# A weight ring of three slots of eight k-tiles, and another split of work between VectorE, ScalarE and GpSimd in the up projection

## What is computed

```python
xn = rmsnorm(x, p['norm_mix_g'])
proj = (xn @ p['w_in'] + p['b_in']).astype(f32)
...   # GLA, mLSTM and RG-LRU branches from slices of proj
mix = (g3[:, :, 0] * (o_gla @ wb[:GLA_V]) + g3[:, :, 1] * (o_m @ wb[GLA_V:GLA_V + M_WIDTH])
       + g3[:, :, 2] * (o_r @ wb[GLA_V + M_WIDTH:]))
x = (x.astype(f32) + mix @ p['w_out'].astype(f32)).astype(dt)
xn2 = rmsnorm(x, p['norm_ffn_g'])
u = (xn2 @ p['w_up']).astype(f32)
uc, fconv_new = causal_dwconv(u, fconv.astype(f32), p['ffn_conv_w'].astype(f32), p['ffn_conv_b'].astype(f32))
u_a, u_b = jnp.split(uc, 2, axis=-1)
x = (x.astype(f32) + (jax.nn.gelu(u_a) * u_b) @ p['w_down'].astype(f32)).astype(dt)
```

## Time and profile before

| | us |
|---|---|
| median of 3 runs (1105.35 to 1109.82) | 1105.7 |
| span of the profiled execution | 1107.9 |
| TensorE busy in it | 1037.6 (94%) |
| VectorE, ScalarE, GpSimd busy | 657.3, 372.1, 346.7 |
| mean granted TensorE clock | 0.978 |
| low parts on GpSimd, 121 of them | 341.2 |
| the two later taps on VectorE, 88 of them | 106.7 |

### The profile page before, as it was taken

One profiled execution on the slowest core, in us unless ns is written; L12 is line 12 of the kernel. 1 busy time (PEld: TensorE's weight loads), 2 busy tenths in 40 slices (PEclk: granted clock), 3 DMA queues, 4 the chain that ended last, 5 costly groups with the idle time before them and its releaser, 6 DMA issues.

```text
span 1107.9 us, 19962 instructions
## 1 busy us (share of the span) xinstructions
PE 1037.6 (94%) x7812; PEld 983.0 (89%) x7812; DVE 657.3 (59%) x1051; ACT 372.1 (34%) x518; POOL 346.7 (31%) x144
## 2 busy tenths in 40 slices
PE   6989999999788999998999999989999999899996
PEld 5979878889787999887999999989999999799995
DVE  4373224457995445657455668888888888531322
ACT  5633333244644454413332332222222222221121
POOL 3333121123221322322342323334433333333330
PEclk9989999999999999999899989999999999999998
DMA  5135212124222222433422322222322223322312
GB/s 152 44 91 124 58 41 66 44 57 114 81 57 58 77 58 58 116 105 95 138 76 69 82 72 76 76 76 78 88 81 84 86 76 90 98 68 84 100 52 81
DMA packets 165766, 89.34 MB, mean 81 GB/s; under 512 B 7508, under 2 KB 163802, under 8 KB 165681
## 3 DMA queue, kind: packets, MB, share of 16 engines
q1 hardware_dynamic: 151493, 79.16, 25.9%
q10 hardware_dynamic: 14222, 9.47, 3.1%
HBM read 82.29 MB, written 6.32 MB: 80 GB/s over the span
## 4 chain that ended last, share of the span: by engine, by line
PE 53%; DVE 25%; issue 13%; POOL 2%; DVEq 2%; ACT 2%; DMA 1%; ACTq 1%; POOLq 0%
PE ps L547 41%; DVE ca L1923 8%; PE ps L536 2%; DVE ca L1919 2%; POOL wlo L495 2%; DVE hp L1931 1%; DVE up L1904 1%; DVE up L1905 1%; PE ps L651 1%; PE ps L647 1%; DVE rt L1688 1%; PE ps L738 1%; PE ps L678 1%; DMA xtok<-x_prompt 1%; PE ps L819 1%
## 5 line engine op out<-in xcount | busy, mean ns | idle before, releaser
L495 POOL TENSOR_TENSOR wlo<-stage,whi 128x1024 fp32r<-128x1024 f32 (+2 forms) x121 | 341.2, 2821 | 734.0 <-ACT whi L1006 452.2
L547 PE MATMUL ps<-xh,whi 128*128 128x272 f32 x1552 | 329.8, 294 | 22.7 <-POOL wlo L495 19.5
L547 PE MATMUL ps<-xh,wlo 128*128 128x272 f32 x1552 | 322.5, 289 | 0.0
L547 PE MATMUL ps<-xl,whi 128*128 128x272 f32 x1552 | 322.4, 289 | 0.0
L547 PEld LDWEIGHTS ps<-xh,whi 128*128 128x128 f32 x1552 | 245.9, 190 | 34.9 <-POOL wlo L495 22.4
L547 PEld LDWEIGHTS ps<-xl,whi 128*128 128x128 f32 x1552 | 246.1, 190 | 0.0
L547 PEld LDWEIGHTS ps<-xh,wlo 128*128 128x128 f32 x1552 | 244.7, 190 | 0.0
L1006 ACT ACTIVATE whi<-stage 128x1024 fp32r<-128x1024 f32 (+2 forms) x59 | 72.4, 1229 | 179.1 <-PE ps L547 175.4
L1923 DVE SCALAR_TENSOR_TENSOR ca<-up,par,ca 128x560 f32<-128x560 f32 x88 | 106.7, 1213 | 12.7
L1015 ACT ACTIVATE whi<-stage 128x1024 fp32r<-128x1024 f32 (+1 forms) x54 | 59.4, 1101 | 77.0 <-PE ps L547 77.0
L547 PE MATMUL ps<-hh,whi 128*128 128x272 f32 x352 | 74.4, 293 | 5.3 <-DVE hl L1935 3.1
(11 more groups left out here) (386 smaller groups left out, 1449.8 us busy)
## 6 DMA issues: line engine op xcount, KB each, us to landing
stage<-w_in SPq DMA_DIRECT2D x52, 512.0 KB, 4.0
stage<-w_up SPq DMA_DIRECT2D x44, 512.0 KB, 3.8
...
stage<-w_out SPq DMA_DIRECT2D x8, 512.0 KB, 3.6
ch<-state_mlstm_C ACTq DMA_DIRECT2D x4, 512.0 KB, 4.2
s_mlstm_C<-ch ACTq DMA_DIRECT2D x4, 512.0 KB, 3.2
...
```

The lines of the kernel that those rows point to most:

```text
L495: pool.tensor_tensor(wlo[:, slot, 0:kt], stage[:, slot, 0:kt], whi[:, slot, 0:kt].bitcast(F32), ALU.subtract).then_inc(s("lo"), 1)
L547: ins = mm(dst[:, r, :], w[:, slot, k0 + k, :], x(k)[:, r * HT:(r + 1) * HT], start=first and k == 0 and q == 0, stop=last and k == n - 1 ...
```

## The change

- `stage`, `whi` and `wlo` have three slots of eight k-tiles in the same space. A load waits for the low part of unit u-3, `hi` until TensorE has used unit u-3 (`used`, `split_made` give the semaphore and value).
- Units of the gated branches become three for two n: two gate units of eight k-tiles, and one with the two branch tiles of four k-tiles side by side (36 units in place of 24). TensorE counts them with `gate_mm` and `br_mm`. On ScalarE `hi` of the next pair's gate stands right behind the gate's sigmoid, ahead of `visit(u, 1)`; `hi` of the branch unit only behind every second n.
- Down projection: units of 8, 8 and 6 k-tiles, three per output tile (24 in place of 16); TensorE waits for `hl` 8, 16, 22.
- Up projection: from the third up unit on, VectorE makes the low parts (`up_lo`, semaphore `lo_up`), and ScalarE the first tap (`first_tap`, an Identity with scale and bias, semaphore `tap0`). VectorE's order in a step is now: evict, `hl` of the step before (r = 0), low part, two taps; then `hp`. ScalarE's is: `hi`, first tap, `gelu`, `hi`, first tap, `up_hi`.
- The first unit's matmuls use 68 weight columns, not 128; the out projection's loops are written out.

The diff, cut to its core:

```diff
 U_SMALL, U_QKV, U_MU, U_RX, U_RY, U_GG, U_MO, U_GB = 0, 1, 9, 13, 17, 21, 25, 29
-U_OUT = U_GB + 3 * KD
+U_OUT = U_GB + 9 * KD // 2
 U_UP = U_OUT + KD
 U_DOWN = U_UP + 2 * NF
-U_END = U_DOWN + 2 * KD
-KT_IN, KT_GB, KT_DOWN, KT_MAX = 8, 12, 11, 12
+U_END = U_DOWN + 3 * KD
+SLOTS, KT = 3, 8
+KT_DOWN = (8, 8, 6)
+U_DVE = U_UP + 2
+N_GB = U_OUT - U_GB
...
 def kt_of(u):
-    return KT_GB if U_GB <= u < U_OUT else KT_DOWN if u >= U_DOWN else KT_IN
+    return KT_DOWN[(u - U_DOWN) % 3] if u >= U_DOWN else KT
+
+
+def used(u):
+
+    if U_GB <= u < U_OUT:
+        i, j = divmod(u - U_GB, 3)
+        return ("gate_mm", 2 * i + j + 1) if j < 2 else ("br_mm", 2 * i + 2)
+    return "gemm", u + 1 - (N_GB if u >= U_OUT else 0)
+
+
+def split_made(u):
+
+    if U_DVE <= u < U_DOWN:
+        return "lo_up", u - U_DVE + 1
+    return "lo", u + 1 - (U_DOWN - U_DVE if u >= U_DOWN else 0)
...
-        stage = at("stage", [P, 2, KT_MAX, P], 0)
-        whi = at("whi", [P, 2, KT_MAX, P], 12288, F32R)
-        wlo = at("wlo", [P, 2, KT_MAX, P], 24576, F32R)
+        stage = at("stage", [P, SLOTS, KT, P], 0)
+        whi = at("whi", [P, SLOTS, KT, P], 12288, F32R)
+        wlo = at("wlo", [P, SLOTS, KT, P], 24576, F32R)
...
-            def free_stage(u):
-
-                sp.wait_ge(s("lo"), u - 1)
...
+            def free_stage(u, more=0):
+
+                if u >= SLOTS:
+                    sem, value = split_made(u - SLOTS)
+                    sp.wait_ge(s(sem), more + value)
...
+                def pair_of_gates(i):
                     for r in range(2):
-                        slot = (u0 + r) % 2
-                        free_stage(i * 2 + (u0 + r))
-                        load(slot, one(gates, i * 2 + r), KT_IN)
-                        sp.dma_start(stage[:, slot, KT_IN:KT_GB], one(outs, i * 2 + r)).then_inc(s(f"branch{slot}"), 16)
+                        free_stage(u0 + r, i * 3)
+                        load((u0 + r) % SLOTS, one(gates, i * 2 + r), KT)
+                    slot = (u0 + 2) % SLOTS
+                    free_stage(u0 + 2, i * 3)
+                    sp.dma_start(stage[:, slot].rearrange("p (k m) c -> p k (m c)", m=2), one(outs, i))\
+                        .then_inc(s(f"stage{slot}"), 16)
...
+            downs = [w_down[q * KT * P:(q * KT + n) * P, :].rearrange("(k p) (m c) -> m p k c", p=P, c=P)
+                     for q, n in enumerate(KT_DOWN)]
...
-            for u0, u1 in ((2, U_GB), (U_GB, U_OUT), (U_OUT, U_DOWN), (U_DOWN, U_END)):
-                with pool.Fori(0, (u1 - u0) // 2) as i:
-                    for r in range(2):
-                        lo(i * 2 + (u0 + r), (u0 + r) % 2, kt_of(u0))
-                if (u1 - u0) % 2:
-                    lo(u1 - 1, (u1 - 1) % 2, kt_of(u0))
+            lo(2, 2, KT)
+            for u0, u1 in ((SLOTS, U_DVE), (U_DOWN, U_END)):
+                with pool.Fori(0, (u1 - u0) // SLOTS) as i:
+                    for r in range(SLOTS):
+                        lo(i * SLOTS + (u0 + r), (u0 + r) % SLOTS, kt_of(u0 + r))
...
+                unit(0, 0, xh, xl, ready="xl", cols=64 + H)
...
+            def gate_and_branch(n, r, hi, lo, more, between, ready=None):
+
+                pe.wait_ge(s("lo"), more + (U_GB + r + 1))
                 if not isinstance(n, int) or n:
                     pe.wait_ge(s("gate_ev"), n)
-                gemm(halves(0), slot, 0, KT_IN, x_of(xh), x_of(xl)).then_inc(s("gate_mm"), 1)
+                gemm(halves(0), (U_GB + r) % SLOTS, 0, KT, x_of(xh), x_of(xl)).then_inc(s("gate_mm"), 1)
                 between()
                 if not isinstance(n, int) or n:
                     pe.wait_ge(s("br_ev"), n)
-                gemm(halves(1), slot, KT_IN, 4, x_of(hi), x_of(lo), ready=ready).then_inc(s("gemm"), 1)
+                if r == 0:
+                    pe.wait_ge(s("lo"), more + (U_GB + 3))
+                gemm(halves(1), (U_GB + 2) % SLOTS, r, 4, x_of(hi), x_of(lo), ready=ready, step=2).then_inc(s("br_mm"), 1)
...
+            with pe.Fori(0, NF // 3) as i:
+                for v in range(6):
+                    pe.wait_ge(s("uev"), i * 6 + (v + 1))
+                    unit(U_DVE + v, v % 2, xh, xl, more=i * 6)
+
+
+            def down(m, dst, hidden=False):
+
+                for q, n in enumerate(KT_DOWN):
+                    if hidden:
+                        pe.wait_ge(s("hl"), KT * q + n)
+                    pe.wait_ge(s("lo"), m * 3 + split_made(U_DOWN + q)[1])
+                    gemm(halves(dst), (U_DOWN + q) % SLOTS, 0, n, x_of(hh, q * KT), x_of(hl, q * KT),
+                         first=q == 0, last=q == 2).then_inc(s("gemm"), 1)
...
+            def hi(u, more=None):
+
+                slot, kt = u % SLOTS, kt_of(u)
+                i, per = (0, 0) if more is None else more
+                act.wait_ge(s(f"stage{slot}"), i * (16 * per // SLOTS) + 16 * (u // SLOTS + 1))
                 if u == 0:
                     act.wait_ge(s("small_in"), 32)
+                if u >= SLOTS:
+                    sem, value = used(u - SLOTS)
+                    act.wait_ge(s(sem), i * (per if sem == "gemm" else 2 * per // 3) + value)
...
+            hi(2)
...
-                hi(u + 2)
+                hi(u + SLOTS)
...
+                hi(U_GB + 3 * i + 3 + r)
                 visit(u, 1)
-                act.wait_ge(s("gemm"), u + 1)
-                hi(u + 2)
+                if r == 1:
+                    hi(U_GB + 3 * i + 5)
                 visit(u, 0)
...
+            def first_tap(j, r):
+
+                act.wait_ge(s("uev"), j * 2 + (r + 1))
+                func(ca[:, r, 0:CONVF], up[:, r, 0:CONVF], ACT.Identity, bias=par[:, bass.ds(j + (P_FB + NF * r), 1)],
+                     scale=par[:, bass.ds(j + (P_FW + NF * r), 1)]).then_inc(s("tap0"), 1)
+
+            def up_step(j, hi_next):
+
+                hi_next(0)
+                first_tap(j, 0)
+                gelu(j)
+                hi_next(1)
+                first_tap(j, 1)
+                up_hi(j)
+
             act.wait_ge(s("ss_mm"), 1)
             func(split(rstd[:]), halves(3), ACT.Sqrt, bias=eps, scale=1.0 / D_MODEL).then_inc(s("std"), 1)
-            hi(U_UP + 2)
-            hi(U_UP + 3)
-            gelu(0)
-            up_hi(0)
-            with act.Fori(1, NF - 1) as j:
-                for r in range(2):
-                    hi_at(j, U_UP + 2 + r, KT_IN)
-                gelu(j)
-                up_hi(j)
-            for r in range(2):
-                hi(U_DOWN + r)
-            gelu(NF - 1)
-            up_hi(NF - 1)
+            with act.Fori(0, NF // 3) as i:
+                for q in range(3):
+                    up_step(i * 3 + q, lambda r: hi(U_UP + SLOTS + 2 * q + r, (i, 6)))
+            up_step(NF - 1, lambda r: hi(U_DOWN + 1 + r))
...
-                def w(t):
-                    return par[:, bass.ds(j + (P_FW + 2 * NF * t + NF * r), 1)]
-
-                out = ca[:, r, 0:CONVF]
-                v.tensor_scalar(out, row[:, 0:CONVF], w(0), par[:, bass.ds(j + (P_FB + NF * r), 1)], ALU.mult, ALU.add)\
-                    .then_inc(s("tap"), 1)
-                for t in (1, 2):
-                    dve.wait_ge(s("tap"), j * 4 + (2 * r + t))
-                    v.scalar_tensor_tensor(out=out, in0=row[:, t:t + CONVF], scalar=w(t), in1=out, op0=ALU.mult, op1=ALU.add)\
-                        .then_inc(s("tap" if t == 1 else "ca"), 1)
-
-            def up_step(j):
-                up_tile(j, 0)
-                up_tile(j, 1)
-                dve.wait_ge(s("gelu"), j + 1)
-                dve.wait_ge(s("ca"), j * 2 + 2)
-                v.tensor_tensor(hp[:, 0:CONVF], ca[:, 0, 0:CONVF], ca[:, 1, 0:CONVF], ALU.mult).then_inc(s("prod"), 1)
...
+            def up_taps(j, r):
+
+                row, out = up[:, r, :], ca[:, r, 0:CONVF]
+                dve.wait_ge(s("tap0"), j * 2 + (r + 1))
+                for k in (1, 2):
+                    w = par[:, bass.ds(j + (P_FW + 2 * NF * k + NF * r), 1)]
+                    if k == 2:
+                        dve.wait_ge(s("tap"), j * 2 + (r + 1))
+                    v.scalar_tensor_tensor(out=out, in0=row[:, k:k + CONVF], scalar=w, in1=out, op0=ALU.mult, op1=ALU.add)\
+                        .then_inc(s("tap" if k == 1 else "ca"), 1)
+
+            def up_lo(u, more=0):
+
+                slot = u % SLOTS
+                dve.wait_ge(s("hi"), more + (u + 1))
+                v.tensor_tensor(wlo[:, slot], stage[:, slot], whi[:, slot].bitcast(F32), ALU.subtract).then_inc(s("lo_up"), 1)
+
+            def hidden_lo(j):
+
                 dve.wait_ge(s("hh"), j + 1)
                 hi_, lo_ = (t[:, bass.ds(j, 1), :].rearrange("p a t -> p (a t)") for t in (hh, hl))
                 v.tensor_tensor(lo_[:, 0:SEQ], hp[:, 0:SEQ], hi_[:, 0:SEQ].bitcast(F32), ALU.subtract)
@@ -1936,11 +1972,30 @@
                                 hi_[:, SEQ:T].rearrange("p (b t) -> p b t", t=LS).bitcast(F32), ALU.subtract)\
                     .then_inc(s("hl"), 1)
 
```

(71 more changed lines are left out.)

179 lines of the change are left out of this document (77 added, 102 removed).

## The result

The changed kernel takes 1072.4 us in the median (1071.9 to 1076.9) against 1107.4 for the kernel before (four runs; its median stood at 1105.7 with three): a ratio of 0.969, interval 0.966 to 0.972. The forecast was 1070, with a range of 1060 to 1086. Its profiled execution has a span of 1069.9 us, against 1107.9 before, so the two traces stand 38.0 us apart, and the medians 34.9; of both kernels the runs scatter by some 5 us.

The account below looks back on a forecast made before the run. TensorE was the floor, waiting in up for low parts because GpSimd's subtractions held VectorE. Terms 22.8 + 7.1 + 1.3 + 4 + 0.5 = 35.7 off 1107.9 gave 1072.2, less 2.2 for the median: 1070 us, range 1060 to 1086.

Parts of the forecast that it names:

- Up projection, 22.8: Up projection: low parts off GpSimd let TensorE set the step, 12.06 us for 13.26, saving 22.8 us.
- Margin, 0.66 us a step: Up projection: a VectorE and ScalarE loop of 11.4 us stays under TensorE's 12.06, leaving 0.66 us per step.
- VectorE bounds: Rival, up projection: VectorE's subtraction takes 2.0 us, not 1.29, so the step is 12.8; 1085 us, chance 0.10.
- Third slot: nothing in up: Up projection: `whi` and `wlo` stand two units ahead, and loads wait three units back; no time gained from the loads.
- Seam, 7.1: Up-to-down seam: waits of 2.17 and 3.10 us go, clock stays at 2.4 GHz for 1.79 more; 7.1 us, else 5.3.
- Out projection, 1.3: End of out projection: last low part moves to VectorE, nothing holds `ssa`, 1.3 us go; at worst 0.
- Gated branches, 4: Gated branches: 36 shorter GpSimd subtractions replace 24, gaining 4 us; bounds a loss of 3 and a gain of 7.
- the branches lose: Rival, gated branches: `whi` moved ahead of state steps lengthens TensorE's chains; 3 us lost, 1077 us, chance 0.08.
- Front, 0.5: Input projection: `whi` one unit earlier saves a short wait, 0.5 us; bounds 0 to 0.6.
- Old pace: Rival, up projection: VectorE, though no longer held, keeps the step at 13.26 us; 1093 us, chance 0.04.
- Tables: Rival, up projection: Identity and Gelu in different tables, three ScalarE loads of 1.28 us per step; 1134 us, chance 0.03.
- no table load in a step: Sign of a right forecast, up projection: ScalarE loads no table within a step.

Follow-up runs that it names:

- the kernels with a moved `whi`: Changed kernel with `whi` behind state steps for n = 3 and 4: 1068.8 us; behind `mh` in mLSTM gates: 1070.5 us; both moves: 1068.8 us.
- The seam kernel: Changed kernel with one wait put back, the first down unit waiting for `hl` 22 instead of `hl` 8: 1082.4 us, ratio 0.979.
- the split on two slots: Kernel before, two slots of 12 k-tiles, only up projection changed: VectorE makes 42 low parts, ScalarE the first tap; 1081.8 us, ratio 0.977.
- the ring alone: Changed kernel keeping three slots, but in up GpSimd makes the low parts and VectorE the first tap again: 1089.2 us, ratio 0.984.

## Why the prediction was right, point by point

- **Total.** The forecast sum was 35.7 us against the profiled execution, and the work from the first unit on became 36.0 shorter. Single terms were off by up to 3 and cancel, so that the total is this close is in part luck.
- **Up projection, 22.8.** Measured 24.5. Cause and bound were right: VectorE held by GpSimd, TensorE the floor at 12.03 (12.06 forecast). Eighteen steps lost 1.23 each, 22.2 us; two others that stood above the floor before (12.9 and 12.3 us) gave 1.1, and a shorter half clock at the start 1.2. That this half clock is shorter for want of the wait for `ssa` is not shown: in two of the kernels with a moved `whi` there is no such wait either, and it lasts 6.8 us, as before the change. The taps of the earlier trace rows did not wait for the whole of GpSimd's instruction, as the prediction has it, but to its end: 3.65 - 1.75 = 1.9 us of 2.62. Two prices were off and did not matter: the subtraction on VectorE took 1.22 (forecast 1.29), the tap on ScalarE 0.86 (0.69).
- **Margin, 0.66 us a step.** The step of the working that failed. It followed one loop through whole durations with a handoff each, and took VectorE for nearly full; VectorE idles 2.1 us a step, and with 1.14 us of taps added it still keeps 12.03. The chance of 0.10 for "VectorE bounds" was too high.
- **Third slot: nothing in up.** Right with low parts on VectorE (266.6 against 266.1), and not shown as a general point: with low parts on GpSimd it is worth 12.5 us, 3.5 of them by the lasting pace. The two halves of the change replace each other here; their separate savings, 17.2 and 24.6 us by the medians, are more than the 34.9 of both.
- **Seam, 7.1.** Measured 7.1. The seam kernel prices it a second time: one wait of 6.9 us costs 9.9.
- **Out projection, 1.3.** Measured 1.4, with a reason that was half of it, as the split on two slots showed. The hold did not vanish: it moved one unit forward (an `ssa` of 2.41 us at 640.57), where units cover it.
- **Gated branches, 4.** Measured 0.9: the mis-sized term. One trace of each kernel gives this to about 1 us only: from the first gate to the mLSTM finish nine traces with this code take 235.6 to 236.9 us, and two with the code of before 237.4 and 237.5, so the gain is 0.5 to 2.0 us, still far from 4. The gain is there up to n = 1: TensorE's wait of 4.06 is 2.54, 2.2 us with the gate ahead. Then it is given back in the way the rival "the branches lose" described, though without the net loss: `whi`, moved ahead of the state steps, delays mLSTM's query by 1.05 us and starts a GpSimd block that holds three convolution taps, 4.47 us for 2.50; and in the mLSTM finish two shorter blocks hold VectorE (2.78 and 2.47 us) in place of one long one (3.89). The rows:

```profile
334.73 4.47 DVE L1474 SCALAR_TENSOR_TENSOR rt<-pm,par,rt 128x568 f32<-128x568 f32 x3
...
346.83 1.05 ACT L1042 ACTIVATE whi<-stage 128x1024 fp32r<-128x1024 f32 x1
347.78 0.61 ACT L1242 ACTIVATE mq<-ps 128x544 f32<-128x544 f32 x1
...
511.50 2.78 DVE L1851 SCALAR_TENSOR_TENSOR mq<-mq,par,mo 128x544 f32<-128x544 f32 x1 [0.45 <-ACT mq L1272]
...
520.12 2.47 DVE L1855 CAST omh<-mq 128x544 fp32r<-128x544 f32 x1
```

  The prediction had counted blocks by their length, and not asked, for each whi that moved, what stands behind it on ScalarE and what VectorE runs when its low part starts.
- **Front, 0.5.** Measured 1.8, outside its bounds of 0 to 0.6: four short waits of TensorE ahead of the first gate shrank or went (the last from 0.64 to 0.16 us). Which part of the change did it was not tried.
- **Down projection, 0.** Measured 0.2.
- **Rivals.** "Old pace" is near what the ring alone gives (13.0). "Tables" was rightly doubted, but for too few reasons: loads did come, 14 of them, from the shape of the loop, and were hidden. The conclusion that there would be no load at all did not hold, nor did "no table load in a step"; that Identity needs none of its own did hold, since one load is left with the same functions in the same order. Where VectorE waits for ScalarE, the loads would have been paid for.
